# Output projections of a two-layer diffusion backbone on one Trainium2 core: column blocks taken by two, tile by tile

## What is computed

```python
for layer in range(2):
    shm, scm, gm, shf, scf, gf = adaln(cond, w_ada[layer], b_ada[layer])   # silu(cond) @ w + b
    h = rmsnorm(y, g_pre_mix) * (1 + scm) + shm
    o = heads(h @ w_att_in) @ w_att_out if layer == 0 else \
        ((hf + hb) * gelu(g)) @ w_rec_out          # xr, g = split(h @ w_rec_in); conv, gates, scans
    y = y + gm * rmsnorm(o, g_post_mix)
    h = rmsnorm(y, g_pre_ffn) * (1 + scf) + shf
    y = y + gf * rmsnorm(relu(h @ w_ff1) ** 2 @ w_ff2, g_post_ffn)
```

## Time and profile before

| | |
|---|---|
| three runs | 2458.65, 2461.57, 2461.56 us; median 2461.56 |
| profiled execution | 2464.59 us, its span in the profile 2462.8 us |
| mean clock granted to TensorE | 0.982 |
| TensorE busy | 2350.9 us, 95% of the span |
| DVE, ACT busy | 1496.8 us (61%), 1122.3 us (46%) |
| read from HBM | 587.76 MB, 240 GB/s over the span |
| stages, from the timeline | attention from 308, att_out to 497, ff2_0 900 to 1283, rec_out 1556 to 1699, ff2_1 2100 to 2463 us |

### The profile page before, as it was taken

One profiled execution on the slowest core, in us unless ns is written; L12 is line 12 of the kernel. 1 busy time (PEld: TensorE's weight loads), 2 busy tenths in 40 slices (PEclk: granted clock), 3 DMA queues, 4 the chain that ended last, 5 costly groups with the idle time before them and its releaser, 6 DMA issues.

```text
span 2462.8 us, 30759 instructions
## 1 busy us (share of the span) xinstructions
PE 2350.9 (95%) x12307; PEld 1828.7 (74%) x12307; DVE 1496.8 (61%) x2055; ACT 1122.3 (46%) x1532; POOL 81.8 (3%) x139
## 2 busy tenths in 40 slices
PE   6999979999999999999999999599999999999998
PEld 2766656678887887787777777466888888777886
DVE  3465744375555566676667778645655555666765
ACT  2433233343334345555553478434444444555554
POOL 2000000000000000000000011000000000000000
PEclk8999989999999999999999999899999999999999
DMA  8899887876777757667677877477756665766553
GB/s 303 308 336 345 306 278 258 300 254 225 248 250 255 263 186 261 208 224 257 204 250 255 280 254 265 171 267 276 240 179 193 186 186 180 251 210 227 196 189 111
DMA packets 305472, 593.23 MB, mean 241 GB/s; under 512 B 20369, under 2 KB 20625, under 8 KB 305073
## 3 DMA queue, kind: packets, MB, share of 16 engines
q1 hardware_dynamic: 299376, 576.90, 68.3%
q0 software_dynamic: 5952, 14.36, 1.9%
HBM read 587.76 MB, written 3.42 MB: 240 GB/s over the span
## 4 chain that ended last, share of the span: by engine, by line
PE 85%; DVE 5%; DMA 4%; ACT 3%; issue 1%; SPq 0%; POOL 0%; DVEq 0%; ACTq 0%; POOLq 0%
PE bank L640 22%; PE bank L630 14%; PE bank L631 14%; PE bank L632 14%; PE bank L642 11%; PE bank L587 6%; DVE w_lo L1246 1%; DMA raw<-in_w_ada 1%; PE bank L778 1%; DMA raw<-in_w_rec_in 1%; DMA raw<-in_w_att_in 1%; PE bank L657 1%; ACT w_hi L954 1%; PE bank L615 1%; DMA raw<-in_w_rec_out 1%
## 5 line engine op out<-in xcount | busy, mean ns | idle before, releaser
L1246 DVE TENSOR_TENSOR w_lo<-raw,w_hi 128x1024 fp32r<-128x1024 f32 x712 | 862.9, 1221 | 446.8 <-ACT w_hi L954 440.9
L954 ACT ACTIVATE w_hi<-raw 128x1024 fp32r<-128x1024 f32 x712 | 744.0, 1053 | 648.7 <-PE bank L642 287.1
L640 PE MATMUL bank<-xt,w_hi 128*128 128x512 f32 x2560 | 912.5, 400 | 4.1 <-DVE w_lo L1246 2.9
L642 PE MATMUL bank<-xt,w_lo 128*128 128x256 f32 x2560 | 716.4, 280 | 0.0
L630 PE MATMUL bank<-w_hi,xt 128*128 128x512 f32 x1568 | 624.0, 398 | 25.6 <-DVE xt L1729 12.0
L631 PE MATMUL bank<-w_lo,xt 128*128 128x512 f32 x1568 | 613.2, 391 | 0.0
L632 PE MATMUL bank<-w_hi,xt 128*128 128x512 f32 x1568 | 612.7, 391 | 0.0
L640 PEld LDWEIGHTS bank<-xt,w_hi 128*128 128x128 f32 x2560 | 480.7, 188 | 157.8 <-issue 32.7
L642 PEld LDWEIGHTS bank<-xt,w_lo 128*128 128x128 f32 x2560 | 482.9, 189 | 0.4
L630 PEld LDWEIGHTS bank<-w_hi,xt 128*128 128x128 f32 x1568 | 295.7, 189 | 154.0 <-issue 45.9
L632 PEld LDWEIGHTS bank<-w_hi,xt 128*128 128x128 f32 x1568 | 295.8, 189 | 63.5
(11 more groups left out here) (183 smaller groups left out, 900.0 us busy)
## 6 DMA issues: line engine op xcount, KB each, us to landing
raw<-in_w_ff SPq DMA_DIRECT2D x512, 512.0 KB, 4.5
raw<-in_w_ada SPq DMA_DIRECT2D x384, 512.0 KB, 6.4
raw<-in_w_att_in SPq DMA_DIRECT2D x72, 512.0 KB, 5.5
raw<-in_w_rec_in SPq DMA_DIRECT2D x64, 512.0 KB, 6.6
raw<-in_w_att_out SPq DMA_DIRECT2D x32, 512.0 KB, 6.8
raw<-in_w_rec_out SPq DMA_DIRECT2D x32, 512.0 KB, 6.7
gain_rows<-in_g_post_mix POOLq DMA_DIRECT2D x8, 256.0 KB, 5.2
gain_rows<-in_g_post_ffn POOLq DMA_DIRECT2D x8, 256.0 KB, 4.9
```

What stands on the lines that cost most here:

```text
L640: nc.tensor.matmul(ps[m][:, :], w_hi[:, h, k, m * P:(m + 1) * P], xt[:, c, :], start=(begin and k == 0), stop=False)
L642: mm = nc.tensor.matmul(ps[m][:, 0:NG * T], w_lo[:, h, k, m * P:(m + 1) * P], xt[:, c, 0:NG * T], start=False, stop=(end and k == 1))
L954: nc.scalar.activation(w_hi[:, n % NSPLIT, :, :], raw[:, T4.p % NRAW, 2 * q:2 * q + 2, :], ACT.Copy)\
L1246: V.tensor_tensor(w_lo[:, n % NSPLIT, :, :], raw[:, T4.p % NRAW, 2 * q:2 * q + 2, :], w_hi[:, n % NSPLIT, :, :].bitcast(fp32), ALU.subtrac ...
```

## The change

The tiles of a sweep with `out == "op"` get an order of their own: blocks 0 and 1 tile by tile, (0,0) (1,0) (0,1) (1,1) and so on; then (2,0), and (2,t) (3,t-1) for each further t, and (3,last). Odd blocks use banks 2 and 3. The rows of ff2 are split with even blocks only. The values of the last heads go to banks 5 and 6, and an order of transfers and queues is new in attention, att_out and rec_out.

```diff
+        elif out == "op":
+            self.order = [(at, t) for t in range(tiles) for at in (0, 1)] + [(2, 0)]
+            self.order += [(2 + k, t - k) for t in range(1, tiles) for k in range(2)] + [(3, tiles - 1)]
...
-    ("att_out", "att_out", "MM" + "A" * 20 + "M" + "AM" * 8 + "AAM" * 2 + "MMM"),
+    ("att_out", "att_out", "AAMAM" + "A" * 17 + "MMM" + "AAM" * 6 + "MMMMM"),
...
-    ("rec_out", "rec_out", "AAM" * 3 + "AM" * 10 + "MMM"),
+    ("rec_out", "rec_out", "MMMMAAMAAM" + "MAAMAAM" * 2 + "AAMAAM" + "MM"),
...
-                BANK_OF.append(2 * (k % 2) if s.deep else 0)
+                BANK_OF.append(2 * (k % 2) if s.deep else 2 * (T4.blk % 2))
...
+        first = next(T4.m for T4 in SEC["att_out"] if T4.kind == "M")
+        ADA_AT[first + 4] = ADA_AT.pop(first + 2)
...
+        VALUE_BANKS = ((3, 2), (3, 2), (3, 2), (5, 6))
...
-                    if s.name == "att_out" and T4.at == 0 and hh == 2:
-                        ada_tile(att_tiles[18])
-                        att_turn_probs(3)
-                        ada_tile(att_tiles[19])
-                        att_values(3)
...
                     main_tile(T4)
+                    if name == "att_out" and T4.at == 0 and T4.t == 0:
+                        pe.wait_ge(heads_ready, 3)
+                    if name == "att_out" and T4.at == 1 and T4.t == 0:
+                        ada_tile(att_tiles[18])
+                        att_turn_probs(3)
+                    if name == "att_out" and T4.at == 0 and T4.t == 1:
+                        ada_tile(att_tiles[19])
+                        att_values(3)
...
-                if T4.s.tiles == 16:
+                if T4.s.tiles == 16 and T4.blk % 2 == 0:
                     c = 2 * h % KC
                     nc.scalar.activation(xt[:, c:c + 2, 0:NG * T], hidden[:, 2 * h:2 * h + 2, :], ACT.Copy)
```

DVE's split has the same condition. In the attention both engines put `split_early("att_out", 4, 6)` (tile (0,1)) between the copies of the last probabilities and the last heads, and DVE stores adaLN sum 12 (`ada_store(ATT_ADA[0])`) before the first maximum instead of two steps later. Behind rec_in_b ACT's queue becomes:

```diff
             flush("rec_in_b")
+            y_rounded(0, 2)
             split_early("rec_out", 2, 4)
             gelu_squares(3)
-            for pair in range(KC // 2):
...
+            y_rounded(2, 4)
+            gelu_tanhs(3)
+            split_early("rec_out", 4, 6)
+            y_rounded(4, 6)
+            split_early("rec_out", 6, 8)
+            y_rounded(6, 8)
```

and DVE's:

```diff
             flush("rec_in_b")
-            split_early("rec_out", 2, 4)
-            gelu_arguments(3)
-            for pair in range(KC // 2):
...
+            y_rest(0, 2)
+            split_early("rec_out", 2, 3)
+            rg_scan(3, 0)
+            split_early("rec_out", 3, 4)
+            y_rest(2, 4)
+            rg_scan(3, 1)
+            gelu_arguments(3)
+            split_early("rec_out", 4, 5)
+            rg_scan(3, 2)
+            split_early("rec_out", 5, 6)
+            y_rest(4, 6)
+            rg_scan(3, 3)
+            split_early("rec_out", 6, 7)
+            outputs(3)
+            split_early("rec_out", 7, 8)
+            y_rest(6, 8)
```

More of the change, by code:

```diff
@@ L49, with __init__ @@
 class Sweep:
[L53 to L57, removed]
+    def __init__(self, name, mode, weight, col0, n, tiles, out, blocks=None):
+        self.name, self.mode, self.weight, self.col0, self.n, self.tiles, self.out, self.blocks = \
+            name, mode, weight, col0, n, tiles, out, blocks
+        self.deep = blocks is not None
+        if self.deep:
+            self.order = [(at, t) for t in range(tiles) for at in range(n)]
+        elif out == "op":
+            self.order = [(at, t) for t in range(tiles) for at in (0, 1)] + [(2, 0)]
+            self.order += [(2 + k, t - k) for t in range(1, tiles) for k in range(2)] + [(3, tiles - 1)]
+        else:
+            self.order = [(at, t) for at in range(n) for t in range(tiles)]
+        self.taken = 0
 class Tile4:
@@ L67, in __init__ @@
         if kind == "M":
-            self.blk = self.s.order[self.at] if self.s.deep else self.at
+            self.blk = self.s.blocks[self.at] if self.s.deep else self.at
             self.begin = self.s.deep or self.t == 0
@@ L107, in plan @@
     S = {s.name: s for s in (
-        Sweep("att_in", "token", w["att_in"], 0, 9, 4, "qkv", order=(6, 7, 8, 0, 2, 4, 1, 3, 5)),
+        Sweep("att_in", "token", w["att_in"], 0, 9, 4, "qkv", blocks=(6, 7, 8, 0, 2, 4, 1, 3, 5)),
         Sweep("att_out", "token", w["att_out"], 0, 4, 4, "op"),
@@ L127, in plan @@
                 s = S[sweep]
[L128 to L131, removed]
+                at, t = s.order[s.taken]
+                s.taken += 1
+                n = token + (at if s.out == "op" else 0) if s.mode == "token" else feature
+                T4 = Tile4("M", len(seq), s=s, at=at, t=t, m=m, sum=n)
                 tiles.append(T4)
                 m += 1
-                if T4.end and s.mode == "token":
+                if T4.end and s.out == "op":
+                    token += s.n if at == s.n - 1 else 0
+                elif T4.end and s.mode == "token":
                     token += 1
@@ L139, in plan @@
         secs[name] = tiles
-    assert all(s.sums == s.n * s.tiles for s in S.values()) and ada == TILE * len(ADA)
+    assert all(s.taken == s.n * s.tiles for s in S.values()) and ada == TILE * len(ADA)
     return S, secs, seq
@@ L713, in last_tiles @@
                                 pe.wait_ge(lo_ready, h + 1)
-                            mm = token_half(0, h % NSPLIT, g, hh, False, T4 is pair[1] and q == 1)
+                            mm = token_half(BANK_OF[T4.sum], h % NSPLIT, g, hh, False, T4 is pair[1] and q == 1)
                             if g == 1:
@@ L978, in token_out @@
                     act.wait_ge(out_read_act, ACT_READS[T4.sum] + g)
-                    nc.scalar.activation(ps[7][:, :], ps[g][:, :], ACT.Square,
+                    nc.scalar.activation(ps[7][:, :], ps[BANK_OF[T4.sum] + g][:, :], ACT.Square,
                                          accum_out=ssq[:, g, T4.blk:T4.blk + 1]).then_inc(out_read_act, 1)
@@ L1044, in gelu_tanhs, with y_rounded @@
                 nc.scalar.activation(gel, gel, ACT.Tanh).then_inc(gelu_tanh, 1)
+            def y_rounded(p0, p1):
+                for pair in range(p0, p1):
+                    act.wait_ge(y_ready, pair // 2 + 1)
+                    nc.scalar.activation(xt[:, 2 * pair:2 * pair + 2, 0:NG * T],
+                                         xc[:, 2 * pair:2 * pair + 2].rearrange("p c g t -> p c (g t)"), ACT.Copy)\
+                        .then_inc(y_hi, 1)
             out_done = set()
@@ L1162, in att_heads @@
                     e = nc.scalar.activation(xt[:, 4 * i:4 * i + 4, g * T:(g + 1) * T],
-                                             ps[3 - g][:, :].rearrange("p (h t) -> p h t", h=4), ACT.Copy)
+                                             ps[VALUE_BANKS[i][g]][:, :].rearrange("p (h t) -> p h t", h=4), ACT.Copy)
                 e.then_inc(heads_hi, 1)
@@ L1190, in _ @@
                     att_scale(i + 1)
+                else:
+                    split_early("att_out", 4, 6)
                 att_heads(i)
```

37 lines of the change are left out of this document (14 added, 23 removed).

## The result

The changed kernel takes **2456.7 us** (median of 20 executions, 2448.2 to 2460.8) against 2461.6 us before: ratio 0.9977, 95% interval 0.9969 to 0.9985. It is faster, by 3.7 to 7.6 us; I had forecast 13.5, and the stated range of 2436 to 2459 us holds the result near its slow edge. In the two profiled executions the span falls by 9.9 us, from 2462.8 to 2452.9 (time of that run: 2454.7).

The account below looks back on a forecast made before the run. TensorE, busy 2350.9 of 2462.8 us, was taken as the bound, with its large waits in rec_out. -2.0 - 16 - 4.5 + 0.6 + 5.3 + 2.1 + 1.0 = -13.5 us gave a median of 2448.1 us, range 2436 to 2459.

Parts of the forecast that it names:

- tile A12.3's landing: Attention head: the adaLN tile, issued earlier in the slot used at 310, lands at 318; -4.5 us (bounds -6 and -1).
- The store moved ahead: Attention head: DVE's store of adaLN columns, ahead of the first maximum, waits for eight small matmuls; +0.6 us on the softmax chain.
- Tail, groups and clock: Attention tail and att_out: late splits +5.3 us, stalls in groups of two adaLN and one main tile +2.1, clock fall +1.0.
- The two new waits: Attention tail: splits of tiles (0,1) and (1,1) queue behind softmax and head copies, idling TensorE 2.1 and 3.7 us.
- a sign of being wrong: Listed as wrong: a w_lo wait over 5 us in rec_out, waits in most att_out groups, or ff2 under clock 1.00.
- ff2 and rec_out: ff2 block ends -2.0 us, fewer splits free; rec_out loss from 35.6 to 19.3 us, so -16 (bounds -8 and -24).
- Rival 1: Rec_out: transfers at 304 GB/s set the pace of the groups, 19 us more, so slower at 2467 us; chance 0.07.
- Rival 2: Rec_out: DVE's queue lasts 38 us as ACT and DVE hand-overs wait; 2456 us, no change that can be told; chance 0.12.
- Rival 3: Landings near the median of 5.3 us, so no group stalls, 13 us less: 2435 us; chance 0.13.
- rival 4: ff2 was paced by the row splits, so halving them gains a tenth of 88 us: 2439 us; chance 0.02.
- Rival 5: Blocks or banks in turn lower TensorE's clock, 73 us if in a tenth of 128 tiles: 2521 us; chance 0.01.
- Rival 6: Rec_out holes come from DVE's y work and return as other waits; gain there nothing, rest +2.5: 2464 us; chance 0.05.

Follow-up runs that it names:

- e5: Changed kernel with the last heads back right behind tile (0,0) and adaLN tile A12.3 transferred ahead of tile (1,0): ratio 0.9937 to the kernel before.
- e8: Changed kernel, last heads and store put back, second main tile transferred later, adaLN and main tiles alternating in att_out and late rec_out, gelu arguments earlier: 2435.3 us, 0.9900.
- e10: Against e8, GpSimd issues the bias rows of adaLN sum 12 ahead of the four cache stores: 2430.6 us, ratio 0.9861 to the kernel before.
- e1: Changed kernel with the attention and att_out of before, keeping the change in rec_out and ff2: 2446.7 us, ratio 0.9925 to the kernel before.
- e3: Kernel before with only ff2_0 and ff2_1 taking blocks by two and half the row splits: ratio 0.9994 to the kernel before.
- e11: The changed kernel measured once more, unaltered: 2456.5 us, ratio 0.9969 to the kernel before.
- e2: Kernel before with only the attention and att_out changed, rec_out and ff2 as before: ratio 1.0036 to the kernel before.
- e12: Changed kernel with only DVE's store of adaLN sum 12 put back behind the first row maximum and copies: 2457.2 us, ratio 0.9974.

## Why the prediction was right in sign and wrong in size

The forecast of 13.5 us was 3.7 to 7.6 in the time and 9.9 in the profiles. The step that failed is the -4.5 us for tile A12.3's landing, which gained some 0.6. By the forecast's own steps:

**The head of the attention failed: forecast -4.5 + 0.6 = -3.9, measured +0.5.** The step was "with tile (1,0) in front and 1.3 MB of cache stores beside I take 318 for its landing (nearest row: 5.3 us median, 11.5 longest)". A12.3 waited 7.62 us and started at 321.09, 10.4 us behind its issue. TensorE was through with it 15.7 us behind the first tile of sum 12 (324.35 - 308.65), in the kernel before 16.3 us (324.49 - 308.20): 0.6 us won by a transfer that was issued some 5 us earlier. Transfers from 305 to 330 and two stretches of the changed kernel:

```profile
raw<-in_w_ada SPq DMA_DIRECT2D x10, 512.0 KB, 11.0
raw<-in_w_att_out SPq DMA_DIRECT2D x2, 512.0 KB, 7.1
```

```profile
310.00:316.00 6.00, 3.47 (x32) 1.89 (x24) 1.29 (x2) 2.00 (x3) 2.40 (x5) 1.00 0.72 201
316.00:322.00 6.00, 0.91 (x4) 0.19 (x4) 2.45 (x2) 1.20 (x2) 0.00 (x0) 0.53 1.05 410
```

SP issued tile (1,0) at 309.78 and A12.3 behind it at 310.70, GpSimd its stores from 309.75. That is 1.05 + 1.05 + 1.3 = 3.4 MB asked for at once. The rate at which they came, all queues together, was slow to rise: 201 GB/s from 310 to 316, so 1.2 MB, and 410 only behind that. The other 2.2 MB take 5.4 us at 410, an estimate of 321.4 for the last of them, and tile A12.3 was issued last. I had set 318, 8 us behind the issue, between a median and a longest landing of quieter stretches, and not from the bytes ahead. The bytes alone would not have mended it: 3.4 MB at 410 GB/s from the issue on also give 318. Both count, the bytes in front (e5, with 1.05 MB less of them, has a head 3.0 us shorter in the profile, though no gain in the time) and the slow start. In e8 and e10, with no main tile in front, the wait is gone.

**The store moved ahead: forecast +0.6, measured 1.2 to 1.9 in the head.** The pieces are small: it delays the row maximum (0.9 us in the two timelines of DVE) and the exponentials (0.4), close to the forecast. What I left out is what TensorE does meanwhile. Freed early, the next adaLN tile is through at 332.8, and then one hole of 3.86 us opens before the second scores in place of two short waits (2.06 and 0.50). Behind it the clock is low and the scores take 4.57 us, 3.46 before (with one exception among the late stores, e1). Stretches and timeline of the changed kernel:

```profile
330.00:335.00 5.00, 2.78 (x25) 1.10 (x23) 3.13 (x5) 2.99 (x14) 0.00 (x0) 1.00 0.80 273
335.00:340.00 5.00, 3.36 (x16) 3.36 (x17) 2.03 (x3) 1.59 (x6) 0.00 (x0) 0.69 0.84 321
```

```profile
336.64 4.57 PE L853 MATMUL bank<-R 128*128 128x128 f32 x24 [3.86 <-ACT R L1159]
...
397.50 0.47 PE L644 MATMUL bank<-w_hi,xt 128*128 128x512 f32 x1 [1.99 <-DVE w_lo L1273]
...
411.04 0.50 PE L644 MATMUL bank<-w_hi,xt 128*128 128x512 f32 x1 [3.63 <-DVE w_lo L1273]
```

**Tail, groups and clock: forecast +5.3 + 2.1 + 1.0 = +8.4, measured +8.5.** The sum is right, its terms less so. The two new waits are 1.99 and 3.63 us, forecast 2.1 and 3.7: the queue positions of the two splits behind the softmax's copies gave them to a tenth. The groups wait 5.2 us in all against 4.4 before, +0.8 for +2.1. Waits in most groups of att_out were named as a sign of being wrong, and they came, in five places, but small. The clock was at 0.66 behind each of the two new waits, not behind one:

```profile
397.00:402.00 5.00, 4.50 (x13) 3.61 (x14) 1.49 (x2) 0.05 (x1) 0.00 (x0) 0.66 1.05 392
411.00:416.00 5.00, 4.96 (x15) 3.90 (x16) 4.00 (x4) 1.57 (x3) 0.51 (x1) 0.66 0.66 211
```

5 us x 0.34, twice, is 3.4 for +1.0. That these two misses cancelled is luck.

**ff2 and rec_out: forecast -18, measured -19.4 in the stages (17 to 18 without the slow rec_out of the one profile before) and -18.5 in e1.** Order and splits of ff2 gave 1 to 2 us together (e3). In rec_out the first matmul waits 2.00 us (forecast 2.3). The y work then leaves TensorE 0.84, 0.81, 0.73 and 0.49 us idle, in four pieces as forecast, but 2.9 us and not 8; yet the clock of 0.89 from 1568 to 1600 costs 3.5 more. (e11, the same kernel, has the clock at 1.00 from 1569 on and 5.8 us of waits in that place, and the stage is the same, 133.8: what a slow clock takes there, the waits give back.) I had not seen that ACT would be only 2.07 us late with its tanh. In the groups 1.06, 0.96, 0.93, 1.23 and 2.83 make 7.0 us, forecast 7.2 and 0.5, but in smaller waits and more of them.

**From the profile to the median: 5.0 us.** I took the profiled execution's 3.0 us above its median as lasting. The changed kernel's was 2.0 below its own. This is no step of the kernel; it is why 9.9 us in the profiles are 4.9 in the medians (7.2 in e11). Of the miss of 8.6 us it is the larger part, 5.0, against 4.4 for the head. Some 2 of the 3.0 us seem to stand in rec_out (140.9 against 138.9 and 139.1 in e2 and e3); why that execution was slow there, no run shows.

**The rivals.** Rival 1 (transfers pace, slower) did not happen in rec_out, which ran at 329 to 331 GB/s, above the 318 from which that rival decided. But its mechanism, bytes over the shared rate, is half of what failed me 1250 us earlier. Rival 2 (DVE's queue of 38 us): from its first y rest at 1569.1 to the end of the last at 1597.4 DVE took 28 us, forecast 30. Rival 3 (no group stalls) fell with the group waits, rival 4 (splits pace ff2) with e3. Rival 5 gets nothing: over blocks and banks in turn the clock stayed at 1.00 (changed kernel and e3); the rules of the Trainium skill, "TensorE: Matmul & The Clock Gate", in the two sections that the prediction names, did not bite here: they tell of an array that idles between its groups of matmuls, and in these stretches it was busy 382.7 of 383 us. Rival 6 (nothing won in rec_out) is excluded by e1.

## What to carry to other kernels

- Where several transfers are issued together behind a pause, take their landings from the bytes ahead in all queues over the rate that the stretch reaches, plus its slow start (some 4 us here: 3.4 MB took 12.6 us from the first issue to the last landing, 8.3 at 410 GB/s), not from a median landing time. And issue what the critical chain needs ahead of the burst, even 8 KB: e10 won 5 to 10 us with that alone.
- Before moving a tile to another place, follow its split slots: who holds them, and behind which instructions on ACT and DVE the next tile's split then stands. Those positions gave two new waits to a tenth of a microsecond.
- A saving of 2 us in one stage of one profile is below what five or six executions can tell: e12's was not seen in the time. And splits taken off engines that TensorE never waits for are worth nothing in time that was seen here.

## What was not expected of the hardware

- The shared rate reached 410 GB/s (316 to 322, DMA share 1.05), above the 385 of the earlier trace rows; the other stretches shown with a share above 1.00 lie between 355 and 407. From 305 to 330 the halves of adaLN tiles, 512 KB each, took 11.0 us in the median from issue to landing, in the kernel before 8.0.
- Behind a pause the rate rises slowly: 201 GB/s in the first 6 us of the burst at 310 (DMA share 0.72), 410 in the next 6.
- A wait as short as 2.0 us may have a low clock behind it, and need not: behind the same 1.99 us the changed kernel shows 0.66 from 397 to 402, and e12 this row:

```profile
397.00:402.00 5.00, 4.84 (x21) 4.04 (x22) 1.15 (x2) 0.00 (x0) 0.00 (x0) 1.00 1.01 368
```

- e11 is like the changed kernel in this, e2 like e12. What decides it, no run here settles. Closing holes gives back clock as well as time: in e10 the first 45 us from 300 on ran at 1.00, where the kernel before has 0.85.
